# A decoder trunk's first weight ring: each 512 KB unit fetched in two transfers of 64 or 128 partitions instead of four of 32 or 64

## The chip, the cores and the metric

The kernel runs on one core of a Trainium2 chip. The metric is the device time in microseconds (us) of one execution. Five engines run their own instruction streams and meet at semaphores: PE (TensorE; its weight loads are shown apart, as PEld), DVE (VectorE), ACT (ScalarE), POOL (GpSimd) and SP (SyncE), which here does nothing but wait and issue DMA transfers ("SPq" in the rows). The transfers themselves are carried by 16 DMA engines.

## What is computed

One decoder layer for 256 tokens of width 2048, all in float32, and a final normalisation:

```
n = rmsnorm(h)
u = n @ w_in                                   # 2048 x 28736
y_a = short_conv_mixer(u_a)        @ w_branch_a
y_b = stick_breaking_attention(u_b) @ w_branch_b
y_c = mamba2_ssd(u_c)              @ w_branch_c
h += (g_a * y_a + g_b * y_b + g_c * y_c) @ w_out
h += peer_ffn(rmsnorm(h))                      # product-key experts: peer_down, peer_up
out = rmsnorm(h)
```

The weights are read once each. Everything that the change touches lies in the products with `w_in`, `w_branch_a`, `w_branch_b`, `w_branch_c` and `w_out`, which are the first half of the program.

## The kernel before

Weights come in units of 512 KB: 128 partitions of 1024 floats. For the first half they pass through a ring, the class `Flow`, of four buffers (`f_raw0` to `f_raw3`, unit n in buffer n mod 4). A unit goes through four hands:

1. SP waits until there is room (`room`: the semaphore `used` must say that unit n-4 has been multiplied), then issues the unit's transfers. Each adds 16 to the buffer's own semaphore `raw_full` when it has landed.
2. ACT waits until all transfers of the unit have landed (`split_hi`, line 132) and writes the rounded high part `f_hi` (line 133).
3. DVE waits for it and writes the rest, `f_lo`, over the raw buffer (`split_lo`, line 138).
4. PE waits for `f_lo` and multiplies. A unit is 16 matmuls in pairs (lines 94 and 95), or 12 matmuls in threes (lines 85, 86 and 87).

There are 608 units, numbered through. The stages, in order of time:

- A, 96 units, and B, 96 units (`a_load`, `b_load`): a unit is four blocks of 128 rows by 256 columns of `w_in`. `pass_load` (line 468) fetches it in four transfers, one for each block of 32 partitions, the highest first: 32 partitions x 4 rows of 1 KB.
- gate and branch stages after A, B and C, and the output product (`branch_load`, and `wide_load`, line 484): two blocks of 128 rows by 512 columns, again four transfers of 32 partitions, 2 rows of 2 KB each.
- C, 160 units in 8 groups of 20 (`c_load`, the loop at line 565). Sixteen units of a group go through `pass_load`. Units 8 to 11 of each group hold two narrow pieces, 128 columns for the matrix called BM and 128 for CM (line 499): four transfers of 64 partitions x 4 rows of 512 bytes.

In the C stage SP has a second task: from unit 17 of one group to unit 4 of the next it also issues one `cs_load` (line 522) behind each unit, a row of `h_scratch` copied to all 128 partitions, 128 KB. In the same stage ACT and DVE work on the group before, in an order that is fixed in the program. At the start of unit 2 of a group ACT has two small operations that form `c_rs` (lines 789 and 792) and wait for a sum by PE (line 1868), and one on `c_ce` (line 777), all ahead of that unit's `f_hi`. Between the `f_hi` of unit 4 and that of unit 5 it loads an activation table and works on `c_xc` (line 751).

All loops on SP, PE, ACT and DVE go over the same units in the same order, so nothing decides the order at run time. The second half of the program (PEER, from 1832 us on) has its own ring and loads, `w_raw`, which the change leaves alone.

Of the kernel before, what the change touches and what calls it, by code (L numbers as in the profile page):

```python
# [11 lines left out]
ds = bass.ds  # L12

P = 128
# [44 lines left out]
def program(nc, x, norm_mix_w, w_in, conv_a_w, ssd_conv_w, ssd_conv_b, ssd_dt_bias, ssd_a_log, ssd_d,  # L59
# [3 lines left out]
    with top:  # L63
# [48 lines left out]
        class Flow:  # L112
# [16 lines left out]

            def split_hi(self, act, n, quads, u, cols):  # L130

                act.wait_ge(self.raw_full[u % 4], (quads + u // 4 + 1) * 64)
                nc.scalar.activation(self.hi[u % 4][:, 0:cols], self.raw[u % 4][:, 0:cols],  # L133
                                     ACT.Copy).then_inc(self.hi_done, 1)

# [9 lines left out]
        fl = Flow()  # L145
# [295 lines left out]
        rows = lambda a, n: a.rearrange("k (c p) -> (k c) p", p=P)  # L441
# [15 lines left out]
        with nc.Block() as block:  # L457
            @block.sync
            def _(sp):
# [3 lines left out]
                    sp.dma_start(dst, src).then_inc(p_vec_in, 16)  # L463

                def pass_load(n, i, cols, rows):
                    for q in (3, 2, 1, 0):
                        at = slice(32 * q, 32 * q + 32)
                        sp.dma_start(fl.raw[i][at, 0:1024].rearrange("p (k n) -> p k n", k=4)[:, :, cols],  # L468
                                     rows.rearrange("(k p) n -> p k n", p=P)[at, :, :]).then_inc(fl.raw_full[i], 16)

                def a_load(it, u):
                    n, i, part = U_AB * it + u, u % 4, A_PASS[u // 4][0]
                    fl.room(sp, n)
                    pass_load(n, i, slice(0, 256), w_in[0, 512 * i:512 * i + 512, ds(COL_A + part * D + it * 256, 256)])

                def b_load(it, u):
                    n, i, part = B0 + U_AB * it + u, u % 4, u // 4
                    fl.room(sp, n)
                    pass_load(n, i, slice(0, 256), w_in[0, 512 * i:512 * i + 512, ds(COL_B + part * D + it * 256, 256)])

                def wide_load(n, u, part):
                    fl.room(sp, n)
                    for q in range(4):
                        sp.dma_start(fl.raw[u % 4][32 * q:32 * q + 32, 0:1024].rearrange("p (k n) -> p k n", k=2),
                                     part.rearrange("(k p) n -> p k n", p=P)[32 * q:32 * q + 32, :, :]
                                     ).then_inc(fl.raw_full[u % 4], 16)

                def c_load(it, u):
                    n, i, r = C0 + UN * it + u, u % 4, u // 4
                    rows = slice(512 * i, 512 * i + 512)  # L490
                    fl.room(sp, n)
                    if r != 2:
                        col = (COL_XS, COL_XS + 256, None, COL_Z, COL_Z + 256)[r]
                        pass_load(n, i, slice(0, 256), w_in[0, rows, ds(col + it * 512, 256)])
                        return
                    for o, col in ((0, COL_BM), (P, COL_CM)):
                        for h in range(2):
                            at = slice(64 * h, 64 * h + 64)
                            sp.dma_start(fl.raw[i][at, 0:1024].rearrange("p (k n) -> p k n", k=4)[:, :, o:o + P],  # L499
                                         w_in[0, rows, ds(col + it * P, P)].rearrange("(k p) n -> p k n", p=P)[at, :, :]  # L500
                                         ).then_inc(fl.raw_full[i], 16)

                def ahead_load(m):
                    if m == 30:
# [21 lines left out]
                def branch_load(base, gate_col, w_branch, kb):  # L526
                    for seg, kind, p, u, m in walk(kb):
                        if kind == "g":
                            wide_load(base + m, m, w_in[0, u * 256:u * 256 + 256, gate_col + p * 512:gate_col + p * 512 + 512])
                        else:  # L530
                            wide_load(base + m, m, w_branch[0, u * 256:u * 256 + 256, p * 512:p * 512 + 512])
                        if base == GC0:
                            cs_load(N_IT - 1, CS_LATE.get(m))
                            ahead_load(m)

                for u in range(U_AB):
                    a_load(0, u)
                    if u in (5, 7, 9, 11):
                        k = 4 * ((u - 5) // 2)
# [22 lines left out]
                for u in range(UN):  # L562
                    c_load(0, u)
                    cs_load(0, CS_EARLY.get(u))
                with sp.Fori(1, N_IT) as it:
                    for u in range(UN):
                        c_load(it, u)
                        cs_load(it - 1, CS_LATE.get(u))
                        cs_load(it, CS_EARLY.get(u))
                branch_load(GC0, COL_G + 2 * D, w_branch_c, KC)  # L570
                for u in range(32):
                    i = u % 8
                    wide_load(O0 + u, u, w_out[0, i * 256:i * 256 + 256, u // 8 * 512:u // 8 * 512 + 512])
# [42 lines left out]
                for tb in range(TB):  # L616
                    for half in range(2):
                        at = slice(half * 1024, half * 1024 + 1024)
# [1769 lines left out]
```

## Time and profile before

| | us |
|---|---|
| median of 3 runs | 3461.89 |
| lowest and highest run | 3459.14, 3465.24 |
| the profiled execution: its time | 3455.88 |
| the profiled execution: span on the core | 3454.2 |
| PE busy in the span | 3399.2 |
| PE weight loads busy | 3014.9 |
| DVE busy | 2248.4 |
| ACT busy | 1775.9 |

The profile is of one execution. What lies outside its span is 3455.88 - 3454.2 = 1.7 us. PE is busy for 98% of the span at a granted clock of 0.999 of full speed. A matmul's end is modelled in this profile and overlaps the next matmul's start, so that a short stop of PE shows better as idle time before a weight load (PEld) than in PE's busy time.

### The profile page before, as it was taken

The page shows a single profiled execution, that of the slowest core. Times are in us where ns is not written, and L with a number is a line of the kernel's source. Part 1 is how long each engine was busy: PE and PEld are TensorE (multiplying, and loading weights), DVE is VectorE, ACT ScalarE, POOL GpSimd, SP SyncE. Part 2 cuts the span into 40 slices and gives each one's busy share as a digit, 9 for nine tenths or more (in the row PEclk, how much of TensorE's full clock was granted, in tenths as well). Part 3 has the DMA queues.
Part 4 walks back from the last instruction along what each step waited for, and adds up shares of the span by engine and source line. Part 5 has one row for each costly group of instructions (what it writes and reads, how often), then busy time and mean ns, then how long its engine had stood idle before and what let it go on. Part 6 is the DMA issues. An engine that isn't in the chain of part 4 may idle for free.

```text
span 3454.2 us, 64264 instructions
## 1 busy us (share of the span) xinstructions
PE 3399.2 (98%) x20477; PEld 3014.9 (87%) x20477; DVE 2248.4 (65%) x2976; ACT 1775.9 (51%) x2708; POOL 6.0 (0%) x24
## 2 busy tenths in 40 slices
PE   8999999999999999999999999999999999999998
PEld 7888889998888888878889999999999988887887
DVE  5665445555567777754556999988889755554555
ACT  4444444444456576564445444357777544444444
POOL 0000000000000000000000000000000000000000
PEclk9999999999999999999999999999999999999999
DMA  8776676566777877768767566665555666667665
GB/s 195 190 189 179 189 186 168 164 165 184 193 188 173 183 176 177 175 176 214 201 179 202 170 183 182 172 173 160 158 160 159 173 193 192 193 193 222 193 194 164
DMA packets 525555, 628.79 MB, mean 182 GB/s; under 512 B 76016, under 2 KB 416464, under 8 KB 524496
## 3 DMA queue, kind: packets, MB, share of 16 engines
q1 hardware_dynamic: 525072, 626.51, 67.3%
q8 instruction: 105, 1.72, 0.2%
q14 instruction: 58, 0.48, 0.0%
q10 hardware_dynamic: 320, 0.08, 0.0%
HBM read 622.03 MB, written 4.26 MB: 181 GB/s over the span
## 4 chain that ended last, share of the span: by engine, by line
PE 91%; DMA 3%; DVE 2%; SPq 2%; ACT 1%; issue 1%; DVEq 0%; ACTq 0%
PE bank L85 22%; PE bank L86 22%; PE bank L87 22%; PE bank L94 14%; PE bank L95 7%; DMA f_raw<-in_w_in 2%; PE bank L1868 2%; PE bank L2278 2%; SPq L468 1%; DVE f_lo L138 1%; ACT f_hi L133 1%; SPq L499 0%; DVE w_raw L1712 0%; DVE w_lo L1719 0%; DMA w_raw<-in_peer_up 0%
## 5 line engine op out<-in xcount | busy, mean ns | idle before, releaser
L138 DVE TENSOR_TENSOR f_lo<-f_raw,f_hi 128x1024 fp32r<-128x1024 f32 x608 | 744.1, 1224 | 726.6 <-ACT f_hi L133 725.4
L133 ACT ACTIVATE f_hi<-f_raw 128x1024 fp32r<-128x1024 f32 x608 | 644.3, 1060 | 871.2 <-DMA f_raw<-in_w_in 633.0
L94 PE MATMUL bank<-xT,f_hi 128*128 128x512 f32 x2560 | 909.1, 399 | 17.0 <-DVE f_lo L138 16.2
L95 PE MATMUL bank<-xT,f_lo 128*128 128x256 f32 x2560 | 714.3, 279 | 0.0
L94 PEld LDWEIGHTS bank<-xT,f_hi 128*128 128x128 f32 x2560 | 480.2, 188 | 144.8 <-DVE f_lo L138 30.4
L85 PE MATMUL bank<-xT,w_hi 128*128 128x256 f32 x2048 | 585.2, 286 | 4.5 <-DVE w_lo L1719 4.5
L87 PE MATMUL bank<-xT,w_lo 128*128 128x256 f32 x2048 | 579.2, 283 | 0.0
L86 PE MATMUL bank<-xT,w_hi 128*128 128x256 f32 x2048 | 579.2, 283 | 0.0
L1806 DVE TENSOR_TENSOR w_lo<-w_raw,w_hi 128x1024 fp32r<-128x1024 f32 x256 | 313.6, 1225 | 340.7 <-PE bank L87 333.2
L95 PEld LDWEIGHTS bank<-xT,f_lo 128*128 128x128 f32 x2560 | 482.4, 188 | 1.3 <-issue 1.1
L85 PE MATMUL bank<-w_hi,u_coef_hi 128*128 128x512 f32 x1024 | 398.6, 389 | 2.8 <-DVE w_lo L1806 2.8
L86 PE MATMUL bank<-w_lo,u_coef_hi 128*128 128x512 f32 x1024 | 398.4, 389 | 0.0
L87 PE MATMUL bank<-w_hi,u_coef_lo 128*128 128x512 f32 x1024 | 398.4, 389 | 0.0
L85 PEld LDWEIGHTS bank<-xT,w_hi 128*128 128x128 f32 x2048 | 392.6, 192 | 5.5 <-DVE w_lo L1719 5.5
L86 PEld LDWEIGHTS bank<-xT,w_hi 128*128 128x128 f32 x2048 | 392.8, 192 | 0.0
L87 PEld LDWEIGHTS bank<-xT,w_lo 128*128 128x128 f32 x2048 | 392.4, 192 | 0.0
L1719 DVE TENSOR_TENSOR w_lo<-w_raw,w_hi 128x1024 fp32r<-128x1024 f32 x256 | 310.0, 1211 | 69.8 <-PE bank L87 67.9
L1094 ACT ACTIVATE w_hi<-w_raw 128x1024 fp32r<-128x1024 f32 x256 | 270.2, 1056 | 162.6 <-PE bank L87 152.5
L997 ACT ACTIVATE w_hi<-w_raw 128x1024 fp32r<-128x1024 f32 x256 | 269.3, 1052 | 114.6 <-PE bank L87 67.0
L1712 DVE STREAM_TRANSPOSE w_raw<-w_raw 128x1024 f32<-128x1024 f32 x256 | 315.9, 1234 | 0.6 <-DMA w_raw<-in_peer_down 0.5
L85 PE MATMUL bank<-f_hi,xT 128*128 128x512 f32 (+1 forms) x768 | 275.0, 358 | 2.6 <-DVE f_lo L138 2.6
L87 PE MATMUL bank<-f_hi,xT 128*128 128x512 f32 (+1 forms) x768 | 271.9, 354 | 0.0
(278 smaller groups left out, 4333.5 us busy)
## 6 DMA issues: line engine op xcount, KB each, us to landing
f_raw<-in_w_in SPq DMA_DIRECT2D x1792, 128.0 KB, 2.8
w_raw<-in_peer_down SPq DMA_DIRECT2D x1024, 128.0 KB, 2.8
w_raw<-in_peer_up SPq DMA_DIRECT2D x1024, 128.0 KB, 2.6
f_raw<-in_w_branch_c SPq DMA_DIRECT2D x256, 128.0 KB, 2.9
f_raw<-in_w_branch_a SPq DMA_DIRECT2D x128, 128.0 KB, 2.8
f_raw<-in_w_branch_b SPq DMA_DIRECT2D x128, 128.0 KB, 2.8
f_raw<-in_w_out SPq DMA_DIRECT2D x128, 128.0 KB, 2.7
w_raw<-in_peer_w_query SPq DMA_DIRECT2D x128, 128.0 KB, 3.0
```

The source lines that it names most:

```text
L85: nc.tensor.matmul(out, lhs[0], rhs[0], start=start, stop=False, skip_group_check=True)
L86: nc.tensor.matmul(out, lhs[0], rhs[1], start=False, stop=False, skip_group_check=True)
L87: return nc.tensor.matmul(out, lhs[1], rhs[0], start=False, stop=stop, skip_group_check=True)
L94: nc.tensor.matmul(both, lhs[0], xT[:, :, k, :], start=start, stop=False, skip_group_check=True)
L95: return nc.tensor.matmul(both[:, 0, :], lhs[1], xT_hi[:, k, :], start=False, stop=stop, skip_group_check=True)
L133: nc.scalar.activation(self.hi[u % 4][:, 0:cols], self.raw[u % 4][:, 0:cols], ACT.Copy).then_inc(self.hi_done, 1)
L138: nc.vector.tensor_tensor(self.lo[u % 4][:, 0:cols], self.raw[u % 4][:, 0:cols], self.hi[u % 4][:, 0:cols].bitcast(F32), ALU.subtract).the ...
L997: nc.scalar.activation(packed(hi[n % 3]), spread(raw[n % NR]), ACT.Copy).then_inc(hi_done, 1)
L1094: nc.scalar.activation(hi[u % 3][:, :], raw[u % NR][:, :], ACT.Copy).then_inc(hi_done, 1)
L1712: v.transpose(raw[n % NR][:, :].rearrange("p (b k c) -> p b k c", b=QUAD, k=8), raw[n % NR][:, :].rearrange("p (b k r) -> p b k r", b=QUAD ...
L1719: v.tensor_tensor(packed(lo[n % 2]), spread(raw[n % NR]), packed(hi[n % 3].bitcast(F32)), ALU.subtract).then_inc(lo_done, 1)
L1806: v.tensor_tensor(lo[u % 2][:, :], raw[u % NR][:, :], hi[u % 3][:, :].bitcast(F32), ALU.subtract).then_inc(lo_done, 1)
```

## The change

Each unit of this ring now comes in two transfers. `pass_load` and `wide_load` take 64 partitions at a time, the upper half first in `pass_load`. The BM and CM pieces each take all 128 partitions in one transfer. What a unit's `raw_full` must reach before ACT may start is accordingly 32 more per round of the ring, not 64. The bytes, the size of each contiguous row (1 KB, 2 KB or 512 bytes), the buffers, the order of the units and everything on the other engines stay.

```diff
-                act.wait_ge(self.raw_full[u % 4], (quads + u // 4 + 1) * 64)
+                act.wait_ge(self.raw_full[u % 4], (quads + u // 4 + 1) * 32)
...
                 def pass_load(n, i, cols, rows):
-                    for q in (3, 2, 1, 0):
-                        at = slice(32 * q, 32 * q + 32)
+                    for h in (1, 0):
+                        at = slice(64 * h, 64 * h + 64)
...
                 def wide_load(n, u, part):
                     fl.room(sp, n)
-                    for q in range(4):
-                        sp.dma_start(fl.raw[u % 4][32 * q:32 * q + 32, 0:1024].rearrange("p (k n) -> p k n", k=2),
-                                     part.rearrange("(k p) n -> p k n", p=P)[32 * q:32 * q + 32, :, :]
+                    for h in range(2):
+                        sp.dma_start(fl.raw[u % 4][64 * h:64 * h + 64, 0:1024].rearrange("p (k n) -> p k n", k=2),
+                                     part.rearrange("(k p) n -> p k n", p=P)[64 * h:64 * h + 64, :, :]
                                      ).then_inc(fl.raw_full[u % 4], 16)
...
                     for o, col in ((0, COL_BM), (P, COL_CM)):
-                        for h in range(2):
-                            at = slice(64 * h, 64 * h + 64)
-                            sp.dma_start(fl.raw[i][at, 0:1024].rearrange("p (k n) -> p k n", k=4)[:, :, o:o + P],
-                                         w_in[0, rows, ds(col + it * P, P)].rearrange("(k p) n -> p k n", p=P)[at, :, :]
-                                         ).then_inc(fl.raw_full[i], 16)
+                        sp.dma_start(fl.raw[i][:, 0:1024].rearrange("p (k n) -> p k n", k=4)[:, :, o:o + P],
+                                     w_in[0, rows, ds(col + it * P, P)].rearrange("(k p) n -> p k n", p=P)
+                                     ).then_inc(fl.raw_full[i], 16)
```

## Rows read from the trace of the kernel before

**Rows 1.** Page, the chain that ended last: shares by engine, then by line.

```profile
PE 91%; DMA 3%; DVE 2%; SPq 2%; ACT 1%; issue 1%; DVEq 0%; ACTq 0%
PE bank L85 22%; PE bank L86 22%; PE bank L87 22%; PE bank L94 14%; PE bank L95 7%; DMA f_raw<-in_w_in 2%; PE bank L1868 2%; PE bank L2278 2%; SPq L468 1%; DVE f_lo L138 1%; ACT f_hi L133 1%; SPq L499 0%; DVE w_raw L1712 0%; DVE w_lo L1719 0%; DMA w_raw<-in_peer_up 0%
```

**Rows 2.** Waits before PE's weight loads: us in total, times, longest.

```profile
PEld bank L94 <- DVE f_lo L138: 30.4, 49, 1.7
...
PEld bank L85 <- DVE f_lo L138: 4.7, 11, 1.8
```

**Rows 3.** The same waits, from 960 to 1500 us alone (C).

```profile
PEld bank L94 <- DVE f_lo L138: 28.7, 46, 1.7
PEld bank L85 <- DVE f_lo L138: 2.3, 2, 1.8
```

**Rows 4.** Timeline of SP in stage A: start, us, transfers issued.

```profile
203.43 1.82 SPq L468 DMA_DIRECT2D f_raw<-in_w_in  x4
206.20 1.82 SPq L468 DMA_DIRECT2D f_raw<-in_w_in  x4
```

**Rows 5.** ACT and DVE on the unit issued at 206.20.

```profile
210.77 1.06 ACT L133 ACTIVATE f_hi<-f_raw 128x1024 fp32r<-128x1024 f32 x1 [2.08 <-DMA f_raw<-in_w_in]
211.87 1.22 DVE L138 TENSOR_TENSOR f_lo<-f_raw,f_hi 128x1024 fp32r<-128x1024 f32 x1 [1.92 <-ACT f_hi L133]
```

**Rows 6.** Stretches of the trace, all engines: us, busy, clock, DMA share, GB/s.

```profile
60.00:278.00 218.00, 218.00 (x1260) 190.50 (x1259) 136.75 (x176) 97.79 (x124) 0.00 (x0) 1.00 0.71 190
960.00:1500.00 540.00, 523.85 (x3107) 443.00 (x3106) 380.68 (x560) 343.06 (x524) 0.00 (x0) 1.00 0.78 179
1059.00:1085.00 26.00, 23.91 (x131) 19.67 (x130) 16.50 (x27) 13.42 (x23) 0.00 (x0) 1.00 1.10 195
```

**Rows 7.** Line 468's transfers in stage A (100 to 250 us): issue, then landing.

```profile
L468 SPq DMA_DIRECT2D f_raw<-in_w_in x216: 316/317/317, 100.8 to 249.5; - x108
...
DMA to landing us min/median/max: 2.4/2.7/3.5
```

**Rows 8.** The same in one stretch with `cs_load` (1062 to 1080 us).

```profile
L468 SPq DMA_DIRECT2D f_raw<-in_w_in x24: 316/317/317, 1061.8 to 1079.0; - x24
...
DMA to landing us min/median/max: 4.3/5.6/6.4
```

**Rows 9.** Line 499: issue ns and landing us, min/median/max, the whole trace.

```profile
L499 SPq DMA_DIRECT2D f_raw<-in_w_in x128: 595/599/1657, 965.8 to 1432.0; - x128
...
DMA to landing us min/median/max: 2.7/2.9/4.2
```

**Rows 10.** Line 540: 128 partitions x 4 rows of 512 bytes, 256 KB a transfer.

```profile
L540 SPq DMA_DIRECT2D dt_w_raw<-in_w_in x4: 434/434/435, 27.9 to 45.2; - x4
...
DMA to landing us min/median/max: 5.4/6.0/6.4
```

**Rows 11.** Timeline of ACT around unit 2 of one group of C.

```profile
1143.54 0.48 ACT L789 ACTIVATE c_rs<-bank,eps_col 128x256 f32<-128x256 f32 x1 [1.75 <-PE bank L1868]
1144.05 0.42 ACT L792 ACTIVATE c_rs<-c_rs 128x256 f32<-128x256 f32 x1
1144.37 1.04 ACT L777 ACTIVATE c_ce<-c_wts 128x1024 f32<-128x1024 f32 x1
1145.32 1.04 ACT L133 ACTIVATE f_hi<-f_raw 128x1024 fp32r<-128x1024 f32 x1
```

**Rows 12.** PE's weight loads at that unit.

```profile
1147.67 0.19 PEld L94 LDWEIGHTS bank<-xT,f_hi 128*128 128x128 f32 x1 [1.72 <-DVE f_lo L138]
```

**Rows 13.** Timeline of ACT, units 0 and 1 of the group before.

```profile
1071.86 1.06 ACT L133 ACTIVATE f_hi<-f_raw 128x1024 fp32r<-128x1024 f32 x1 [2.33 <-DMA f_raw<-in_w_in]
1075.25 1.06 ACT L133 ACTIVATE f_hi<-f_raw 128x1024 fp32r<-128x1024 f32 x1 [2.33 <-DMA f_raw<-in_w_in]
```

**Rows 14.** Timeline of SP: BM and CM units of two groups.

```profile
1098.89 2.94 SPq L499 DMA_DIRECT2D f_raw<-in_w_in  x4
1102.08 2.94 SPq L499 DMA_DIRECT2D f_raw<-in_w_in  x4
...
1163.93 2.44 SPq L499 DMA_DIRECT2D f_raw<-in_w_in  x2
```

**Rows 15.** Waits before PE's weight loads, 1160 to 1180 us.

```profile
PEld bank L94 <- DVE f_lo L138: 1.0, 3, 0.4
```

## The prediction

> **What bounds the kernel now.** I read the chain that ended last first [rows 1]. PE holds 91% of it; the DMA transfers of `f_raw` from `w_in` hold 2%, SP's line 468 1%. So the part of the program that a change to the loads can touch at all is a few per cent. I asked next how long PE really stands still for this ring. Before its weight loads it waits for `f_lo` 30.4 + 4.7 = 35.1 us in all [rows 2], and 28.7 + 2.3 = 31.0 us of that lies between 960 and 1500 us, in stage C [rows 3]. Outside it 4.1 us are left, for nearly all of the other 448 units. The stretches say the same: from 60 to 278 us PE is busy for the whole 218 us, in C 523.85 of 540 [rows 6].
>
> Why is stage A free of waits? SP gets room and issues a unit every 206.20 - 203.43 = 2.77 us, which is PE's time for a unit [rows 4]. The unit issued at 206.20 has landed at 210.77, 4.6 us later; ACT takes 1.06 us, and DVE is done at 211.87 + 1.22 = 213.1, 6.9 us after room [rows 5]. PE comes to it three units after room, at 3 x 2.77 = 8.3 us. So there are 1.4 us to spare. A unit may land 1.4 us later, or any amount sooner, without PE's noticing.
>
> In C the reserve is used up. In a stretch with `cs_load` (a burst, below: eight units, from unit 17 of a group to unit 4 of the next, seven times) the DMA share is 1.10 against 0.71 in A, at 195 against 190 GB/s [rows 6], and a transfer lands after 5.6 us instead of 2.7 [rows 7, 8]. SP is not what is late there: its issues still take 317 ns each. The DMA engines have a backlog. ACT starts on unit 0 at 1071.86 and on unit 1 at 1075.25, 3.4 us apart, each time released by the DMA, where 2.77 would do [rows 13].
>
> **What part of the 31 us can move.** Not the wait at unit 2. ACT stands for 1.75 us until PE's sum is there, does 0.48, 0.42 and 1.04 us of other work, and only then comes to the `f_hi` of the unit [rows 11]; PE stops for 1.72 us [rows 12]. No load ended that chain. It comes once in each of seven groups: 7 x 1.7 = 12 us. Left are 31 - 12 = 19 us in C and 4 outside, 23 us as the ceiling of any gain (0.7% of the time).
>
> **The change, part by part.**
>
> *Issue on SP, lines 468 and 484.* Four transfers take 1.82 us from the first to the end of the last [rows 4]; one is 0.317 us [rows 7], so they follow each other at (1.82 - 0.32) / 3 = 0.50 us, 0.18 of it registers. A 64-partition transfer with four rows each took 0.599 us [rows 9], a 32-partition one 0.317 [rows 7]. I take 0.599, the row with the same partitions and row count: two transfers then take 0.60 + 0.18 + 0.60 = 1.4 us, and the second starts 0.78 us after the first where the fourth started at 1.5. At the lower price, 0.317, it would start at 0.5. Either way SP has less to do, and outside C it has 0.9 us to wait at each unit already: worth nothing there.
>
> *Landing.* Before: 1.5 us to the last issue and 2.7 to its landing [rows 7], 4.2 after room. After: no row has 256 KB on 64 partitions. From below, 0.78 + 2.4, the quickest landing of half the bytes, 3.2 us. From above, 0.78 + 6.4, the slowest 256 KB transfer [rows 10], 7.2; that one stood behind a whole unit in the queue. The 512 KB are the same rows of memory and have to be moved in any cut. In A 190 GB/s is only what is asked; in the burst, with the engines full, it is hardly more [rows 6]. So I take 4.2 us after room, unchanged, with 3.7 to 4.7 as the likely spread. In A, B and the gate stages all of that is inside the 1.4 us of reserve: 0 us. At the upper bound it would not be: 7.2 + 2.3 = 9.5 against 8.3, and each 0.1 us beyond costs a quarter of it per unit over 608 units, 15 us.
>
> Here a rule can be weighed. The Trainium skill, "SBUF — State Buffer", section "Door 1: The DMA port swizzle", says that partitions 0 to 63 reach no more of the memory's ports than 0 to 31, so a 64-partition transfer gets the bandwidth of a 32-partition one. By that rule a unit's data moves at the same rate before and after, and the sum is the one above. The same page, "The DMA setup-cost knee", prices a transfer at 2 us plus its bytes at 436 GB/s, 2.6 us for 256 KB; by that estimate the second would land at 0.78 + 2.6 = 3.4 us, 0.8 sooner than now. For 128 KB it gives 2.3 us where the trace has 2.7, so here it is on the quick side, and its gain would be hidden outside C too.
>
> *The bursts.* The data in the queue stays, 512 KB of the unit and 128 KB of `cs_load`, five transfers of overhead become three. Bounds: nothing, or the whole excess of 3.4 - 2.77 = 0.6 us a unit. With the DMA share at 1.10 and no SP wait to take away I stay near the first: 0.05 us a unit, and the lateness that has built up over six units falls by 0.3 us. 7 x 0.3 = -2 us.
>
> *BM and CM units.* Issuing one takes 2.94 us [rows 14], more than PE's 2.77; SP falls behind by itself over four units. After, two transfers of the form of line 540, 0.434 us each [rows 10]: 0.43 + 0.18 + 0.43 = 1.05 us, 1.9 less. Landing was 2.94 - 0.6 + 2.9 = 5.2 us after room [rows 9]; after, 0.61 + 2.9 to 0.61 + 6.4, and I take 4.2 as for the others. The wait there is 1.0 us in the group from 1160 us [rows 15], and it is less or nothing in others; half of that on average, all recovered, is 0.5 x 7 = -3.5 us at best. I take -1.5, because part of each such wait comes from ACT and DVE, whose work is unchanged.
>
> *Stray long issues.* Now and then one issue takes up to 1.7 us [rows 9]: from 1163.93 two transfers of line 499 took 2.44 us instead of 0.60 + 0.18 + 0.60 = 1.38, 1.1 us lost, and PE waits shortly behind it [rows 14, 15]. Half the issues should meet this less often, in places with no reserve: -0.5 us, between 0 and -3. The start (first 60 us) has short waits of the same kind: -0.5.
>
> Sum: 0 - 2 - 1.5 - 0.5 - 0.5 = -4.5 us. Against the profiled execution that is 3455.9 - 4.5 = 3451.4. That execution is 6.0 us below the median of the runs, and the same step from the median gives 3461.9 - 4.5 = 3457.4 us.
>
> **The rivals.**
>
> *Nothing moves, because every wait in C is the backlog or ACT (same time, 3461).* For it: ACT's and DVE's fixed order at units 2 and 5. Against: SP's 2.94 us per BM and CM unit, which is plainly over PE's time. It differs from my forecast by less than can be measured; a change of under 0.2%, 6.9 us, is about what a measurement of this kernel cannot tell from none. I hold the two together.
>
> *The bursts drain faster than by their bytes (faster, 3449).* If what fills the DMA engines is the count of transfers and not the bytes, two fifths of it goes, and the 3.4 us between units falls towards 2.9. Then the waits at units 19, 0, 1, 3, 4 and 5 shrink to a third: of the 19 us about 12 come back, 3461.9 - 12 - 0.5 = 3449. For it: 195 GB/s in the burst is hardly above the 190 of stage A though the engines are full, so it is not bytes alone. The Trainium skill, "DMA: Bandwidth & Descriptors", section "Rules for kernel authors", is on this side: it asks for coalesced transfers and one of 128 partitions in place of two halves.
>
> *The last piece of a unit lands later (slower, 3471).* ACT needs the whole unit. Where the fourth small transfer now has little left to do when it is issued, the second large one has 256 KB of its own. If a unit lands 0.7 us later than now, 4.9 after room, stages A and B still hide it, but C has no reserve: two waits per group (the end of the burst and unit 5) grow by 0.7, and so does the start, 7 x 1.4 = 10 us, 3471. It decides against the change from about 0.5 us of lateness on. The Trainium skill, "Perfetto Trace Analysis", section "DMA Optimizations", states the rule behind it: splitting lets some of the work start sooner when the DMA engines are mostly idle. They are 0.71 busy in A [rows 6], so the trace is only half on its side. Past 1.4 us of lateness A and B would pay too, and the time would go over 3480.
>
> **How the numbers follow.** My forecast together with the first rival: 0.59. The fast rival: 0.26. The slow one: 0.15, of which 0.03 past 1.4 us. The likeliest is 3457.5. The range leaves out the ends of the fast case (all 19 us back, 3443) and of the slow one: 3446 to 3471. Faster by over 0.2% means under 3455, slower over 3468.8; the chances are those of the cases.
>
> **What the changed profile would show.** Right: two issues per unit of about 0.6 us each, in A the whole unit landed 3.7 to 4.7 us after room; `f_lo` waits outside C still near 4 us; BM and CM units at 1.05 us of SP each with no wait behind them; the waits at unit 2 unchanged at 1.7; the sum in C near 27 us instead of 31. Wrong: landings in a burst clearly below 3.4 us apart (fast rival), or ACT released by the DMA more than 4.7 us after room in stage A (slow rival). A change of the granted clock or of PE's pace per matmul would be something that I have no reason for.

## The result, and the profile after

| | before | after |
|---|---|---|
| median of 12 runs each, us | 3462.6 | 3475.14 |
| lowest and highest run, us | 3453.28, 3467.21 | 3468.05, 3482.64 |
| the profiled execution: time, span, us | 3455.88, 3454.2 | 3481.1, 3479.3 |

The ratio is 1.0038, with a 95% interval of 1.0028 to 1.0047: 12.5 us slower, between 10 and 16. The forecast was 3457.5, with a range that ended at 3471. It was wrong, on the side of the slow rival.

The profiled execution of before lies 7 us below the median of its runs, that of after 6 us above. So the two spans differ by 25 us where the medians differ by 12.5. The traces below show places; what a place costs is taken from the medians.

The page of after, the chain that ended last, by engine and by line; and of its list of DMA issues the row of `w_in` (count, KB each, median us to landing):

```profile
PE 89%; DMA 5%; DVE 3%; ACT 2%; issue 1%; SPq 1%; DVEq 0%; ACTq 0%
PE bank L85 21%; PE bank L86 21%; PE bank L87 21%; PE bank L94 14%; PE bank L95 7%; DMA f_raw<-in_w_in 4%; PE bank L1866 2%; PE bank L2276 2%; DVE f_lo L138 1%; ACT f_hi L133 1%; SPq L468 0%; DMA w_raw<-in_peer_up 0%; DVE w_raw L1710 0%; ACT L749 0%; DVE w_lo L1717 0%
...
f_raw<-in_w_in SPq DMA_DIRECT2D x896, 256.0 KB, 4.1
```

Beside [rows 1] the transfers of `w_in` went from 2% of the chain to 4%, SP's own line from 1% to 0%. SP has less to do, the end of the transfers comes later.

Waits before PE's weight loads (us, times, longest), the whole trace of after:

```profile
PEld bank L94 <- DVE f_lo L138: 39.8, 55, 2.0
...
PEld bank L85 <- DVE f_lo L138: 11.3, 22, 1.8
```

And from 960 to 1505 us alone (stage C):

```profile
PEld bank L94 <- DVE f_lo L138: 37.1, 52, 1.7
...
PEld bank L85 <- DVE f_lo L138: 2.3, 2, 1.8
```

PE waits 51.1 us for `f_lo` where it waited 35.1 [rows 2]. In C it is 39.4 against 31.0 [rows 3]: 8.4 us more. The other half of the growth, 51.1 - 39.4 = 11.7 against 4.1, lies outside C. That makes 16 of the 25 us between the spans. Of the other 9, some 2 us are more short "issue" waits at line 94, 2 us a longer wait of a PEER weight load (5.0 against 3.2), and about 4 us lie in stage A, where PE has no idle time in either trace. Its matmuls are a little longer in the trace of after. From 100 to 250 us, first before, then after (times, busy us, mean ns of one):

```profile
L94 PE MATMUL bank<-xT,f_hi 128*128 128x512 f32 x434 | 150.5, 394 | 0.0
L94 PE MATMUL bank<-xT,f_hi 128*128 128x512 f32 x426 | 150.6, 399 | 0.0
```

The granted clock is 1.00 in both stretches, the full 2.4 GHz. A unit takes PE 2.77 us in the one and 2.83 us in the other. This is not the change: the traces of rest_64 and rest_64_padb below, with stage A cut as in after, are at 2.77, and those of c_halves_128 and one_128, with stage A cut as before, are at 2.83. What sets it is not known. Last, the granted clock was at the lower of its two levels (0.50, 1.2 GHz) from 1556.5 to 1559.8 and from 3205.2 to 3208.4 us, after PE had stood for 2.2 and for 5.0 us. At half the speed that is worth at most 3 us, an estimate, and it is the 0.998 against 0.999.

Three stretches of after, to be held against [rows 6] (us, PE, PEld, DVE, ACT, POOL, clock, DMA share, GB/s):

```profile
60.00:278.00 218.00, 218.00 (x1236) 188.86 (x1235) 134.54 (x173) 96.40 (x125) 0.00 (x0) 1.00 0.78 185
100.00:250.00 150.00, 150.00 (x851) 130.04 (x850) 92.12 (x118) 66.02 (x85) 0.00 (x0) 1.00 0.78 186
960.00:1500.00 540.00, 517.63 (x3072) 435.95 (x3070) 378.74 (x552) 333.81 (x508) 0.00 (x0) 1.00 0.84 176
```

Stage A still has PE busy for all 218 us. But the DMA engines are 0.78 busy there instead of 0.71, and they move no more (185 against 190 GB/s, as PE asks for less at 2.83 us a unit). In C the share is 0.84 instead of 0.78, at fewer GB/s. The same bytes hold the engines for longer. This is the row that the forecast had left no room for. The share of one and the same cut differs between executions too: in stage A it is 0.66 to 0.71 in the five traces with the cut of before. In stage B PE has the same pace in all of them and in after, which makes it the better place to compare. From 600 to 750 us, before, then after:

```profile
600.00:750.00 150.00, 150.00 (x995) 138.12 (x994) 78.43 (x95) 68.22 (x86) 0.00 (x0) 1.00 0.60 165
600.00:750.00 150.00, 150.00 (x996) 138.12 (x995) 78.57 (x95) 67.71 (x85) 0.00 (x0) 1.00 0.69 164
```

Line 468's transfers of after in stage A, 100 to 250 us: issue ns (min/median/max), then landing.

```profile
L468 SPq DMA_DIRECT2D f_raw<-in_w_in x107: 598/599/627, 99.6 to 249.5; - x107
...
DMA to landing us min/median/max: 3.6/4.0/4.3
```

An issue takes 0.599 us, as taken. The second starts 0.60 + 0.18 = 0.78 us after the first and, at the median of 4.0 here or of 4.1 for all of `w_in`, the unit has landed 4.8 to 4.9 us after room. Before it was 1.5 + 2.7 = 4.2 [rows 4, 7]. (Taken unit by unit in the same stretch, from the first issue to the last landing, the medians are 4.96 and 4.34 us: both a little more, and as far apart.)

### The profile page after: what moved, and what is told of

It reads as the page before. It is cut to its first block, busy times and chain, and to the rows that moved or that the text cites. A ratio compares the mean times of both kernels' runs of the same rounds, so it can differ in the third digit from the quotient of the medians.

```text
span 3479.3 us, 61768 instructions
## 1 busy us (share of the span) xinstructions
PE 3411.5 (98%) x20477; PEld 3017.8 (87%) x20477; DVE 2251.2 (65%) x2976; ACT 1778.2 (51%) x2708; POOL 6.0 (0%) x24
## 4 chain that ended last, share of the span: by engine, by line
PE 89%; DMA 5%; DVE 3%; ACT 2%; issue 1%; SPq 1%; DVEq 0%; ACTq 0%
PE bank L85 21%; PE bank L86 21%; PE bank L87 21%; PE bank L94 14%; PE bank L95 7%; DMA f_raw<-in_w_in 4%; PE bank L1866 2%; PE bank L2276 2%; DVE f_lo L138 1%; ACT f_hi L133 1%; SPq L468 0%; DMA w_raw<-in_peer_up 0%; DVE w_raw L1710 0%; ACT L749 0%; DVE w_lo L1717 0%
```

## The experiments

The kernels describe a unit's transfers by lists of pieces (first and end partition, first and end row of the four that a partition gets); SPLIT_A, SPLIT_B and SPLIT_C are for the ordinary units of the stages, SPLIT_W for `wide_load`, SPLIT_M for each half of a BM and CM unit. All else is as in the kernel before, unless said otherwise. `pass_load` stands at line 482 in them. Where a unit lands is worked out as above: the start of the last issue after the first, plus the median landing. The diffs are against the kernel before, and show only the cut.

**The change in three parts.** Three kernels that together make up the change: the ordinary units of C alone (c_pass_64), everything but C's units and the BM and CM ones (rest_64), and BM and CM alone (bmcm_128b).

```diff
-for q in (3, 2, 1, 0):                                # C's ordinary units
-    at = slice(32 * q, 32 * q + 32)
+SPLIT_C = [(64, 128, 0, 4), (0, 64, 0, 4)]            # A, B, W, M as before
```

> Only the sixteen ordinary units of each group of the C stage come in two transfers of 64 partitions; A, B, the gate and branch stages, the output product and the BM and CM units are as before. Theory (the unit lands 0.7 us later, and only C has no reserve for that): most of the loss is here, 9 us of the 12.5, so 3470 to 3473 us, with the waits for f_lo in C at 43 us or more instead of 31. Rival (the loss is spread over all stages): about 4 us, 3466.

Measured: 3474.01 us, ratio to before 1.0039 (1.0026 to 1.0053), +12.5 us. The wait rows from 960 to 1510 us of its trace:

```profile
PEld bank L94 <- DVE f_lo L138: 35.0, 53, 1.7
...
PEld bank L85 <- DVE f_lo L138: 3.1, 3, 1.8
```

38.1 us of waits instead of 31.0, in an execution that was the quickest of its five (3464.98 us). The time is 1 us above the expected 3470 to 3473, the waits are below the expected 43. The lateness of 64-partition units is paid in C, and it alone is as large as the whole loss.

The second part:

```diff
+SPLIT_A = [(64, 128, 0, 4), (0, 64, 0, 4)]
+SPLIT_B = [(64, 128, 0, 4), (0, 64, 0, 4)]
+SPLIT_W = [(0, 64, 0, 2), (64, 128, 0, 2)]            # C and M as before
```

> The other part alone: A, B, gate and branch stages and the output product in two transfers of 64 partitions, everything in C as before. Theory (these stages hide a unit that lands at 4.9 us instead of 4.2 after room): at most 4 us, from the start and the gate stage behind C, 3463 to 3467 us, landing 4.9 us after room in A. Rival (spread loss): 8 us and more, 3470 or above.

Measured: 3490.96 us, 1.0089 (1.0075 to 1.0103), +29 us, more than twice the whole change. No theory of mine had that. Its trace shows something else than late units. The chain that ended last, around one jump back of the loop over C's groups (line 579):

```profile
1343.71 0.04 SPq L579
1343.76 4.19 issue
1347.95 0.06 SPq L579
```

And ACT soon after:

```profile
1352.88 1.06 ACT L133 ACTIVATE f_hi<-f_raw 128x1024 fp32r<-128x1024 f32 x1 [5.39 <-DMA f_raw<-in_w_in]
```

SP has jumped, and does nothing for 4.19 us. It comes to the next unit 4 us late, and ACT stands for 5.39 us. The loop has 7 rounds and so 6 jumps back, and each of them has such a stop, 3.8 to 4.6 us long and 24.7 us in all. None of the other twelve traces has one. PE's longest wait for `f_lo` in C is 3.5 us instead of 1.8, and the mean granted clock is lower there:

```profile
60.00:278.00 218.00, 218.00 (x1259) 190.59 (x1258) 137.13 (x176) 97.29 (x126) 0.00 (x0) 1.00 0.79 189
1100.00:1200.00 100.00, 95.11 (x583) 80.70 (x583) 73.73 (x111) 60.19 (x93) 0.00 (x0) 0.98 0.68 165
1300.00:1400.00 100.00, 95.38 (x564) 81.51 (x564) 69.34 (x104) 65.65 (x102) 0.00 (x0) 0.97 0.67 168
1354.50:1361.30 6.80, 6.05 (x19) 5.18 (x19) 3.28 (x5) 1.06 (x1) 0.00 (x0) 0.50 1.06 206
```

The means of 0.98 and 0.97 come from short stretches like the last one, at the lower level of 1.2 GHz; five of the six stops have one behind them.

The cut of A's units cannot reach into C's loop, whose instructions are those of before. What differs is where these instructions stand in SP's program, since fewer transfers go ahead of them. The next kernel (rest_64_padb) tests that: rest_64 with 216 waits added that are always met already, so that the loop stands elsewhere again. (The aim was the place of before modulo 256 instructions. By the instructions that SP's traces list, the loop stands 424 earlier than before in rest_64 and 208 earlier in rest_64_padb, so it was not met by that count, and nothing here shows that 256 matters.)

```diff
+                        if base == GB0:
+                            for _ in range(6):
+                                sp.wait_ge(p_vec_in, 16)
...
+                    if u < 12:
+                        for _ in range(4):
+                            sp.wait_ge(p_vec_in, 16)
```

> The same as rest_64, with extra waits in SP's program that are always met, 216 more instructions between the B stage and the C loop, so that the C loop stands in SP's program at the same place modulo 256 as in the kernel before. In rest_64 SP stood for about 4 us at the jump back of the C loop in six of seven rounds, with a weight unit late behind it. If that stop comes from where the loop's code lies (code theory), it is gone here, the jump takes 0.2 us again, and the time is 3464 to 3470. If it comes from the 64-partition transfers themselves, the time stays near 3490.

Measured: 3468.55 us, 1.0017 (1.0008 to 1.0026), +6.1 us. More instructions, and 22 us less than rest_64. SP's timeline over the same jump:

```profile
1338.77 1.82 SPq L482 DMA_DIRECT2D f_raw<-in_w_in  x4
1340.77 0.35 SPq L536 DMA_DIRECT2D c_wts<-h_scratch  x1
1341.59 1.82 SPq L482 DMA_DIRECT2D f_raw<-in_w_in  x4
```

```profile
960.00:1500.00 540.00, 522.15 (x3103) 441.87 (x3102) 381.15 (x560) 340.99 (x521) 0.00 (x0) 1.00 0.78 178
```

From `cs_load` to the next unit it is now 1341.59 - 1341.12 = 0.5 us, and the clock in C is 1.00. So the 4 us stop, and with it 22 of rest_64's 29 us, goes away when instructions are added ahead of the loop. That it hangs on where the loop's code stands is the reading that fits; one pair of kernels is all that bears on it. What SP does in these 4 us the trace does not say. The remaining 6 us are what the 64-partition cut costs outside C.

The third part, BM and CM:

```diff
-for h in range(2):                                    # each half of a BM and CM unit
-    at = slice(64 * h, 64 * h + 64)
+SPLIT_M = [(0, 128, 0, 4)]                            # all else as before
```

> Only the BM and CM units change: one transfer of 128 partitions for each piece, two for a unit. Theory (the parts add up, and this one works the other way): SP has 1.9 us less to issue at each of the four units and the unit lands sooner, so C loses 1 to 4 us: 3457 to 3461 us. Rival (this part is worth nothing, as ACT is behind there): within 0.1% of the kernel before.

Measured: 3459.06 us, 0.9987 (0.9978 to 0.9996), -3.4 us. From 960 to 1500 us of its trace:

```profile
PEld bank L94 <- DVE f_lo L138: 23.6, 34, 1.7
...
PEld bank L85 <- DVE f_lo L138: 2.5, 2, 1.8
```

26.1 us of waits instead of 31.0. The three parts add to 12.5 + 6.1 - 3.4 = +15.2, against 12.5 measured for all of them, which is within their intervals.

**Which property of the cut.** Each transfer of 64 partitions differs from its forerunner in three ways: it is larger, it is the last of two, and it covers another set of partitions. The following kernels pull these apart.

The same two transfers of 256 KB, but each over all 128 partitions with half of the rows (halves_128):

```diff
+SPLIT_A = SPLIT_B = SPLIT_C = [(0, 128, 2, 4), (0, 128, 0, 2)]
+SPLIT_W = [(0, 128, 0, 1), (0, 128, 1, 2)]
+SPLIT_M = [(0, 128, 0, 4)]
```

> Two transfers of 256 KB for each unit as in the changed kernel, but each over all 128 partitions with half the rows. If a transfer on 64 partitions is slow because of the partitions that it covers (partition theory), a unit lands at 4.2 us or sooner after room in A, the DMA share in A falls from 0.78 to 0.71 or less, and the time is at or under 3462. If what counts is that the last piece holds 256 KB (grain theory), it lands at 4.9 us as in the changed kernel and the time is 3472 to 3478.

Measured: 3441.68 us, 0.9949 (0.9935 to 0.9962), 18 us faster than before in its own comparison, and by the medians 33 us faster than the change. From 100 to 250 us:

```profile
L482 SPq DMA_DIRECT2D f_raw<-in_w_in x108: 368/373/373, 100.9 to 248.5; - x108
...
DMA to landing us min/median/max: 2.7/2.9/3.1
```

```profile
100.00:250.00 150.00, 150.00 (x867) 131.10 (x866) 93.98 (x121) 66.82 (x86) 0.00 (x0) 1.00 0.63 189
```

The unit has landed 0.373 + 0.18 + 2.9 = 3.5 us after room. A transfer of 256 KB, issued last, is not late: it is 1.1 us quicker than one of the same size over 64 partitions. The share of the DMA engines is 0.63 for 189 GB/s, where rest_64 with its 64-partition transfers has 0.79 for the same 189 (its row above). PE's waits for `f_lo` are 14.6 us in the whole trace:

```profile
PEld bank L94 <- DVE f_lo L138: 11.5, 11, 1.7
...
PEld bank L85 <- DVE f_lo L138: 3.1, 4, 1.8
```

Four transfers of 128 KB, as before, but each over 64 partitions with half of the rows (quarters_64):

```diff
+SPLIT_A = SPLIT_B = SPLIT_C = [(64, 128, 0, 2), (64, 128, 2, 4), (0, 64, 0, 2), (0, 64, 2, 4)]
+SPLIT_W = [(0, 64, 0, 1), (0, 64, 1, 2), (64, 128, 0, 1), (64, 128, 1, 2)]
```

> Four transfers of 128 KB again, but each on 64 partitions with half the rows (BM and CM as before). Partition theory: late all the same, 4.9 us or more after room in A, the time 3472 or more. Grain theory: the last piece is small, 4.2 to 4.5 us after room (the issues take longer, 2.9 us for four if each takes 0.6), the time 3462 to 3467.

Measured: 3572.78 us, 1.0325 (1.031 to 1.0339), +111 us.

```profile
L482 SPq DMA_DIRECT2D f_raw<-in_w_in x186: 598/599/615, 99.5 to 249.9; - x186
...
DMA to landing us min/median/max: 2.6/2.8/3.1
```

```profile
100.00:250.00 150.00, 141.84 (x742) 112.97 (x743) 80.16 (x103) 57.38 (x74) 0.00 (x0) 1.00 0.60 161
```

A transfer of half the rows costs SP the same 599 ns. A unit then holds SP for 4 x 0.78 = 3.1 us, PE needs one every 2.77, and SP bounds the whole first half: PE is busy for 141.84 of 150 us even in A. Both times failed: the expectation itself had 2.9 us for four issues of 0.6, and I did not hold that against PE's 2.77. The unit lands 3 x 0.78 + 2.8 = 5.1 us after room, mostly by its issues. As a test of how fast the data moves it says little: 161 GB/s are asked, not 189.

The last transfer made small again: 256 KB over 64 partitions, then two of 128 KB over 32 (last_smallb). The BM and CM units of this kernel are those of the changed kernel, although the expectation says that they are as before:

```diff
+SPLIT_A = SPLIT_B = SPLIT_C = [(64, 128, 0, 4), (32, 64, 0, 4), (0, 32, 0, 4)]
+SPLIT_W = [(0, 64, 0, 2), (64, 96, 0, 2), (96, 128, 0, 2)]
+SPLIT_M = [(0, 128, 0, 4)]
```

> Three transfers for each ordinary unit: 64 partitions first, then 32 and 32; BM and CM as before. Grain theory: the last piece is as small as before, so the unit lands at 4.2 to 4.3 us after room and the time is that of the kernel before. Partition theory: the three move at the pace of one half at a time all the same, 4.3 to 4.7 us, 3462 to 3470.

Measured: 3470.93 us, 1.0026 (1.0017 to 1.0035), +8.5 us.

```profile
L482 SPq DMA_DIRECT2D f_raw<-in_w_in x161: 316/463/634, 99.4 to 250.0; - x161
...
DMA to landing us min/median/max: 3.2/3.5/4.0
```

```profile
100.00:250.00 150.00, 150.00 (x851) 130.12 (x850) 91.94 (x118) 65.89 (x84) 0.00 (x0) 1.00 0.76 186
```

The three issues take 0.60, 0.46 and 0.32 us at the median, so the last one starts 0.60 + 0.18 + 0.46 + 0.18 = 1.4 us after the first, and 1.4 + 3.5 = 4.9 us after room the unit is there: as late as with two large ones, although its last piece is as small as before the change, and later than either theory had it. With halves_128 this refutes the reason that the slow rival gave. The share of the DMA engines stays high, at 0.76. Since the BM and CM units give back about 3.4 us here as they do in the change, the ordinary units cost about 8.5 + 3.4 = 12 us, an estimate from two runs. The kernel is not plainly faster than the change: 1.0026 (1.0017 to 1.0035) against 1.0038 (1.0028 to 1.0047).

Four transfers of 32 partitions as before, only in another order, so that neighbours in the queue come from different halves of the partitions (inter_32b):

```diff
-for q in (3, 2, 1, 0):
+for q in (3, 1, 2, 0):                                # wide_load: 0, 2, 1, 3
```

> The kernel before with the same four transfers of 32 partitions for each ordinary unit, in another order: 3, 1, 2, 0 (and 0, 2, 1, 3 in the wide units), so that neighbours in the queue lie in different halves of the partitions. Partition theory (two transfers to the same half share a path, two to different halves overlap): a unit lands under 4.2 us after room and the time falls by 3 to 15 us, 3447 to 3459. Grain theory: no difference, 3461.

Measured: 3448.08 us, 0.996 (0.9946 to 0.9974), -14 us, with no byte, size or count changed.

```profile
DMA to landing us min/median/max: 2.3/2.5/2.8
```

```profile
100.00:250.00 150.00, 150.00 (x851) 130.03 (x851) 91.16 (x117) 65.85 (x86) 0.00 (x0) 1.00 0.66 186
960.00:1500.00 540.00, 529.64 (x3164) 452.60 (x3165) 387.93 (x568) 348.08 (x530) 0.00 (x0) 1.00 0.68 183
```

Landed 1.5 + 2.5 = 4.0 us after room. In C the DMA share is 0.68 where it was 0.78 [rows 6]. The 0.66 of stage A proves nothing by itself: c_halves_128 below leaves stage A as before and has the same there:

```profile
100.00:250.00 150.00, 150.00 (x851) 130.03 (x850) 92.27 (x118) 65.88 (x84) 0.00 (x0) 1.00 0.66 185
```

The time is the proof, 14 us by the order alone, so what is in work at the same time counts, and this holds for the kernel before too. I read that as the partitions. One rival stands untested: partition p of a unit always takes the rows p, 128 + p and so on of the weights, so every kernel here that changes which partitions are filled together also changes which rows of memory are read together. It is at least no matter of one matrix: the pages give a transfer of 256 KB from `w_out` 4.2 us to landing in after and 3.3 in halves_128, with 4.1 and 3.0 for `w_in`.

**How far it goes, and what is the best count.** Only C's ordinary units over 128 partitions (c_halves_128):

```diff
+SPLIT_C = [(0, 128, 2, 4), (0, 128, 0, 2)]            # A, B, W, M as before
```

> Only the sixteen ordinary units of each group of C come in two transfers of all 128 partitions and half the rows; everything else is as in the kernel before. Theory (the gain of halves_128, like the loss of the changed kernel, is made in C, where no reserve hides a landing): 3443 to 3449 us, and waits for f_lo in C of 14 to 18 us. Rival (the gain is spread over the stages): 3452 or more.

Measured: 3449.07 us, 0.9963 (0.9949 to 0.9976), -13 us, as expected. ACT's starts on a unit in a burst:

```profile
1062.31 1.06 ACT L133 ACTIVATE f_hi<-f_raw 128x1024 fp32r<-128x1024 f32 x1 [4.00 <-DMA f_raw<-in_w_in]
1065.19 1.06 ACT L133 ACTIVATE f_hi<-f_raw 128x1024 fp32r<-128x1024 f32 x1 [0.87 <-DMA f_raw<-in_w_in]
1067.98 1.06 ACT L133 ACTIVATE f_hi<-f_raw 128x1024 fp32r<-128x1024 f32 x1 [1.19 <-DMA f_raw<-in_w_in]
```

They are 2.9 and 2.8 us apart, PE's pace, where before they were 3.4 [rows 13]. Now the burst of after, first ACT, then line 468 from 1062 to 1087 us:

```profile
1078.23 1.06 ACT L133 ACTIVATE f_hi<-f_raw 128x1024 fp32r<-128x1024 f32 x1 [1.81 <-DMA f_raw<-in_w_in]
1081.60 1.06 ACT L133 ACTIVATE f_hi<-f_raw 128x1024 fp32r<-128x1024 f32 x1 [2.30 <-DMA f_raw<-in_w_in]
1084.99 1.06 ACT L133 ACTIVATE f_hi<-f_raw 128x1024 fp32r<-128x1024 f32 x1 [2.33 <-DMA f_raw<-in_w_in]
```

```profile
L468 SPq DMA_DIRECT2D f_raw<-in_w_in x14: 598/599/647, 1065.8 to 1084.6; - x14
...
DMA to landing us min/median/max: 4.0/6.1/7.2
```

Still 3.4 us apart, each start released by the DMA: three transfers instead of five bring no relief, wider ones do. The pace within a burst is that of before, so the change does not lose there. That units which land 0.7 us later go into the burst with that much less in hand is how I read the loss.

Four transfers of 128 partitions, one row each, in A, B and C (rows_128):

```diff
+SPLIT_A = SPLIT_B = SPLIT_C = [(0, 128, 3, 4), (0, 128, 2, 3), (0, 128, 1, 2), (0, 128, 0, 1)]
```

> A, B and C in four transfers of 128 KB as before, but each over all 128 partitions with one row (wide, BM and CM units as before). Partition theory: the bytes move as fast as in halves_128 and only the last issue comes later, so about 4.0 us after room in A, DMA share near 0.63, and 3440 to 3450 us. If two large pieces are themselves what makes halves_128 fast, this one stays near 3461.

Measured: 3442.43 us, 0.9951 (0.9938 to 0.9965). An issue takes 333 ns, a transfer lands after 2.2 us, the unit 3 x 0.51 + 2.2 = 3.7 us after room; the DMA share in A is 0.67.

One transfer of 512 KB a unit in B, C and `wide_load` (one_128):

```diff
+SPLIT_B = SPLIT_C = [(0, 128, 0, 4)]
+SPLIT_W = [(0, 128, 0, 2)]
+SPLIT_M = [(0, 128, 0, 4)]
```

> One transfer of 512 KB over all 128 partitions for each unit of B, C and the wide stages, two for BM and CM, A as before. Partition theory: 16 engines with the whole unit at once, landed 3.5 to 4 us after room in B, 3438 to 3446 us. If the size of the last piece counts beside the partitions, it lands later than the 3.5 us of halves_128, by 0.3 us or more, with no effect on the time outside C.

Measured: 3445.53 us, 0.9951 (0.9938 to 0.9965). In B (600 to 750 us) one issue of 373 ns and 3.7 us to landing. One, two or four transfers over all partitions land 3.5 to 3.7 us after room, and their times cannot be told apart. All three beat both the kernel before and the change.

## Why the prediction was wrong

**What bounds the kernel, and the ceiling.** Right. The waits lay where the argument had them. The ceiling of 23 us for any gain, 31 us in C less the 12 at unit 2 and 4 outside, is borne out by halves_128: it took 18 to 20 us, and left 14.6 us of waits, of which 7 x 1.7 = 12 are those at unit 2 [rows 11, 12] (the seventh stands behind C, at the same place in the gate stage).

**Issue on SP.** Right: 599 ns was measured. It is also the price for 64 partitions with half of the rows, so the row with the same partitions was the one to read. The 317 ns for before holds for line 468 alone: in `wide_load`, line 484, the median issue took 427 ns. That does not change the sum.

**Landing: the step that failed.** "The 512 KB are the same rows of memory and have to be moved in any cut. [...] So I take 4.2 us after room, unchanged." They landed 4.8 to 4.9 us after room. The bytes are the same, but not the time that the DMA engines need for them. In stage B, where PE asks for 164 to 165 GB/s in each of these traces, their share is 0.69 over 64 partitions and 0.60 over 32 in order (both rows stand above). With the halves alternating (inter_32b) and over 128 (halves_128) it is:

```profile
600.00:750.00 150.00, 150.00 (x995) 138.18 (x994) 77.22 (x93) 68.99 (x88) 0.00 (x0) 1.00 0.57 165
600.00:750.00 150.00, 150.00 (x995) 138.12 (x994) 78.12 (x95) 68.84 (x87) 0.00 (x0) 1.00 0.54 164
```

(The 0.57 is a small step from before: c_halves_128, with B as before, has 0.58.) The step took the spread of 3.7 to 4.7 as a matter of queueing alone, and entered it as 0 us in the sum.

The slow rival had the right lateness, 4.9, and the right places: hidden in A, paid in C. Its sum, 10 us, stands against +12.5 (9 to 18) for C's units alone, and +6 (3 to 9) for the rest. Its reason was wrong: last_smallb has a small last piece and is as late, halves_128 has a large one and is early. So the rival was worth more than its 0.15, but no row of before gave the ground for it.

The Trainium skill, "SBUF — State Buffer", section "Can I just issue two DMAs to hit both halves?", says that all 16 ports are reached only by one transfer over all 128 partitions. The runs with such transfers agree (landing 2.9 instead of 4.0 us for 256 KB). I had drawn from that page's section "Door 1: The DMA port swizzle" only that 64 partitions are no better than 32, and concluded "the same rate before and after". By that section's table, partitions 0 to 31 and 64 to 95 reach different ports; that alternating the halves gains 14 us agrees with it. The section on two DMAs says that transfers to the two halves serialize, and gives 6% more bandwidth for two at once. Here the landing of a transfer in stage A fell from 2.7 to 2.5 us with the halves alternating, a gain of about that size, and the kernel gained 14 us by it.

What no run explains is why one transfer of 64 partitions is slower than two of 32 from the same half one behind the other. In the change and before it the order is upper half, then lower half, and the share still rises from 0.60 to 0.69 in stage B. That stays open.

**Inside A, B and the gates: 0 us.** Right for A, where PE never waits for a unit (its slower pace in that trace is not the change's doing, as said above). Too round elsewhere: outside C the waits grew by 7.6 us in the trace of after. Most of it, 6.9 against 1.8 us, lies behind 1510 us, in the last branch and output products, and 1.5 us between 700 and 960, where there was none. I had read the reserve of 1.4 us from one stage and used it for all.

**The bursts: -2 us.** Wrong. Units in a burst still came 3.4 us apart. The fast rival's premise, that the count of transfers fills the engines, is refuted by the same row. Its effect exists: with 128 partitions the units come 2.8 to 2.9 us apart, and 13 us come back from C alone.

**BM and CM: -1.5 us.** Right in its mechanism, and rather small. SP issues such a unit by two transfers of 373 ns, 0.373 x 2 + 0.18 = 0.93 us instead of 2.94 [rows 14]; measured -3.4 us, between -1 and -8. Line 497's transfers in after, the whole trace:

```profile
L497 SPq DMA_DIRECT2D f_raw<-in_w_in x64: 367/373/1587, 973.8 to 1446.1; - x64
...
DMA to landing us min/median/max: 2.9/3.2/4.9
```

They landed 0.55 + 3.2 = 3.8 us after room, not 4.2. This was the change's only good part, and its only part over 128 partitions. How much of the gain is SP's shorter issuing and how much the 128 partitions no run separates.

**Stray long issues and the start: -1 us.** Nothing of it can be seen. The first 60 us have 2.5 us of `f_lo` waits instead of 1.7, and issues of 1.6 us still occur in line 497.

In sum: the bursts' -2 did not come, BM and CM gave 2 us more than taken, and the landing, entered as 0, was +12.5 in C and +6 outside it.

## What to carry to other kernels

When a load is cut differently, ask which partitions each transfer covers before asking how many there are or how large: here the same bytes kept the DMA engines 0.54 to 0.69 busy in stage B, and 512 KB landed 3.5 to 4.9 us after room. A DMA share that rises at the same GB/s is the sign to look for, in a stretch where the consumer has the same pace in both traces. Fewer issues on an engine that waits anyway bring nothing, and a lateness hidden in one stage is paid in the next that has no reserve, so the reserve must be read stage by stage.

## What the runs showed of the hardware

- An issue on SP is not priced by bytes, and does not grow evenly with partitions. With rows of 1 KB it took 317 ns for 32 partitions, 599 ns for 64 (with four rows or two), 373 ns for 128 with two rows or four, 333 ns for 128 with one. It is no fixed price either: a 32-partition issue directly behind a 64-partition one took 463 ns in last_smallb, and one with rows of 2 KB 427 ns in `wide_load`.
- One loop of SP stood for about 4 us at each of its six jumps back in rest_64, and at none with 216 instructions added ahead of it. PE was busy for 95 of 100 us in these stretches, against 98.6 (1300 to 1400 us) where the stop was gone. The granted clock went to its lower level of 1.2 GHz behind five of the six stops.
- With C's ordinary units in two transfers over all 128 partitions, the units of a burst came 2.8 to 2.9 us apart, the row of `cs_load` included: 640 KB each time. Over 32 in order or over 64 partitions the same took 3.4 us.
- At a granted clock of 1.00 and without a wait, the same matmuls of stage A took PE 2.77 us a unit in seven traces and 2.83 in five, whatever the cut (quarters_64, where SP bounds stage A, is left out).
